# A hybrid convolution decoder layer: from three token blocks in 2 phases to two token blocks in 16 phases, with its long convolution, its PSUM use and its transposes rewritten

## The reference

```
u = rmsnorm(h) * g_mix
proj = u @ w_in                         # 1024 -> 9 x 1024, in this order:
a_b, a_c, a_h, a_z, b_v, b_g, b_z, gate_a, gate_b
s  = a_c * a_h
ya = (a_b * dwconv3(s) * silu(a_z)) @ w_out_a
v  = b_v * sigmoid(b_g)
c  = dwconv31(v) + b_conv_b             # causal, each channel for itself
yb = (silu(layernorm(c)) * silu(b_z)) @ w_out_b
m  = sigmoid(gate_a) * ya + sigmoid(gate_b) * yb
h  = h + m @ w_o
h  = h + sigmoid(rmsnorm(h) @ w_pg) * (p @ w_pe)
y  = rmsnorm(h) * g_final
```

## Time and profile before

| | us |
|---|---|
| three runs | 1177.35, 1189.94, 1219.92 |
| median | 1189.94 |
| span of the profiled execution, slowest core (core 4) | 1170.0 |
| span of the fastest core (core 7) | 1132.5 |
| TensorE busy (share) | 927.0 (79%) |
| VectorE, ScalarE, GpSimd busy (share) | 512.3 (44%), 295.8 (25%), 257.2 (22%) |
| 16 DMA engines: GpSimd's queue, SyncE's queue | 50.9%, 24.7% |

### The profile page before, as it was taken

The page is one execution under the profiler, slowest core; times in us unless marked ns, Lnnn a source line. Parts: engine busy times, 40 slices in busy tenths (PEclk is TensorE's granted clock), DMA queues, the critical chain, the costliest instruction groups (busy, mean ns, idle before and its releaser), DMA issues.

```text
span 1170.0 us, 17595 instructions; the slowest of 8 cores (1132.5 to 1170.0 us)
## 1 busy us (share of the span) xinstructions
PE 927.0 (79%) x6138; PEld 542.0 (46%) x6156; DVE 512.3 (44%) x673; ACT 295.8 (25%) x400; POOL 257.2 (22%) x544
## 2 busy tenths in 40 slices
PE   0799997989866679998898972367768875899995
PEld 0355554645432345555464630124445553566542
DVE  1336556553234433556455231144254653453244
ACT  2122221431143312222242121133111121331143
POOL 3123231222111122222122110011442531111011
PEclk9899998989987898999899996579898897788887
DMA  8999997797522279999899999422899998563001
GB/s 148 188 183 186 177 190 127 120 139 123 92 91 108 87 124 150 165 168 128 95 111 101 99 62 36 112 96 85 146 164 187 172 190 134 89 102 62 1 36 77
DMA packets 101813, 141.98 MB, mean 121 GB/s; under 512 B 42592, under 2 KB 52832, under 8 KB 100704
## 3 DMA queue, kind: packets, MB, share of 16 engines
q0 software_dynamic: 47200, 82.69, 50.9%
q1 hardware_dynamic: 54528, 58.17, 24.7%
HBM read 208.10 MB, written 16.84 MB: 192 GB/s over the span
## 4 chain that ended last, share of the span: by engine, by line
PE 56%; DMA 13%; DVE 12%; issue 6%; ACT 5%; another core or an unknown queue 3%; POOL 2%; SPq 2%; DVEq 0%; POOLq 0%; ACTq 0%
PE ps L467 41%; DMA vd<-t_vt 7%; PE ps L813 5%; DMA t_reg<-vd 4%; PE ps L773 3%; PE ps L575 2%; ACT t_junk L339 2%; PE ps L806 2%; DVE t_reg L831 1%; DVE t_reg L828 1%; SPq L548 1%; DVE t_tmp L696 1%; PE ps L443 1%; DVE t_tmp L700 1%
## 5 line engine op out<-in xcount | busy, mean ns | idle before, releaser
L467 PE MATMUL ps<-t_uT,t_ring 128*128 128x384 bf16 (+1 forms) x3456 | 577.7, 329 | 31.1 <-DVE t_vkeep L532 17.8
L467 PEld LDWEIGHTS ps<-t_uT,t_ring 128*128 128x128 bf16 x3456 | 347.0, 101 | 253.3 <-issue 53.9
L319 POOL DMA_DIRECT2D t_ring<-w_in x216 | 115.3, 538 | 358.2 <-PE ps L467 304.0
L443 PE MATMUL ps<-t_idb,t_xn 128*128 128x128 bf16 x136 | 16.7, 300 | 127.6 <-ACT t_xn L436 94.9
L467 PE MATMUL ps<-t_cbuf,t_ring 128*128 128x384 bf16 (+1 forms) x384 | 70.2, 339 | 9.7 <-DVE t_cbuf L730 9.7
L342 POOL TENSOR_SCALAR t_msq<-t_ssq 128x1 f32<-128x1 f32 x51 | 9.7, 190 | 307.6 <-ACT t_junk L339 307.3
L443 PEld LDWEIGHTS ps<-t_idb,t_xn 128*128 128x128 bf16 x136 | 13.0, 136 | 133.5 <-issue 133.5
L575 PE MATMUL ps<-t_reg,t_ring 128*32 128x384 bf16 (+2 forms) x1024 | 40.0, 311 | 43.4 <-DMA t_reg<-vd 43.4
L737 ACT ACTIVATE t_tmp<-ps 128x768 f32<-128x768 f32 (+1 forms) x48 | 37.1, 772 | 146.2 <-PE ps L467 146.2
L813 PE MATMUL ps<-t_wpg_t,t_u2T 128*128 128x512 bf16 x268 | 73.5, 433 | 0.3
L745 DVE SCALAR_TENSOR_TENSOR t_tmp<-t_tmp,ps 128x768 f32<-128x768 f32 (+1 forms) x30 | 27.3, 910 | 105.2 <-PE ps L467 105.2
(11 more groups left out here) (87 smaller groups left out, 889.7 us busy)
## 6 DMA issues: line engine op xcount, KB each, us to landing
t_ring<-w_in POOLq DMA_DIRECT2D x216, 256.0 KB, 8.9
t_xs<-x SPq DMA_DIRECT2D x34, 512.0 KB, 4.5
y<-t_reg SPq DMA_DIRECT2D x17, 512.0 KB, 2.6
t_ring<-w_cv POOLq DMA_DIRECT2D x24, 256.0 KB, 8.5
t_ring<-w_oa POOLq DMA_DIRECT2D x24, 256.0 KB, 9.8
t_ring<-w_ob POOLq DMA_DIRECT2D x24, 256.0 KB, 6.1
vd<-t_vt SPq DMA_DIRECT2D x16, 200.0 KB, 6.4
t_reg<-vd SPq DMA_DIRECT2D x32, 100.0 KB, 5.6
```

The costliest lines, as they stand in the source:

```text
L319: S.add("pool", lambda e, k=k, src=src: e.dma_start(out=ring[k][:, :], in_=src), reads=after, writes=[f"ring{k}"], dma=f"ring{k}")
L443: S.add("pe", lambda e, i=i, k=k, b=b: e.transpose(out=psb[:, b, k * 128:(k + 1) * 128], in_=xn[i][:, k * 128:(k + 1) * 128], identity=idb ...
L467: S.add("pe", lambda e, b=b, k_=k_, k=k, rhs=rhs, si=si: e.matmul(ps[:, b + si, 0:n], lhsT=ring[k_][:, 128 * k:128 * k + 128], rhs=rhs(k, si),
```

## The change

The program is new; the arithmetic is that of the reference as before.

- **Two blocks** of 1024 and 1152 tokens (the second holds the 128 sample tokens). A unit is 16 matmuls of 512 columns, and in the second block 8 more of 128 columns. All weights are read twice. `unit_u` (operand `uT`) does one chunk of columns after another; `unit_w` (operands `yaT`, `yb`) runs the chunks innermost.
- **PSUM slots**: three of two banks in the first block, two of three banks in the second; banks 6 and 7 are the convolution's. Part of the VectorE work is put in a list (`bg`) and issued in batches by `drain`.
- **16 phases**: a prompt token's place in its block is (token mod 16, token div 16). `vd` has 16 x 128 rows of 66 values (132 bytes), in the second block of 114 (228 bytes), instead of 2 x 128 rows. It comes back in three DMAs of 32 partitions, 64 groups long.
- **Long convolution**: for each pair of channels one matmul with 96x32 weights over 64 columns, 64 of them for a chunk in four column groups; in the second block 64 more over 32 columns for the sample tokens. Each needs no accumulation. Its weights (96 rows of 8 KB in f32) have two buffers of their own, loaded on GpSimd's queue. The result goes through 32x32 transposes on VectorE.
- **Layer norm statistics**: 8 matmuls on quarter tiles, short VectorE and ScalarE work, then one DMA to DRAM and two that broadcast it back to all partitions.
- **Last stage**: apart from the first tile of a block, `u2T` is made by a DMA transpose on SyncE's queue, and so is `uT` of the second block. The products with `w_o` run two tiles ahead. The factor `g_ple` is put into `w_pg`, `g_mix` into the scaling. The last tile of all is done in halves.
- **Start**: eight x tiles are loaded; the weight loads past the third wait for the eighth of them, ahead of the norms' operations on GpSimd's queue. Two units run tile by tile while `uT` is being made.
- **`hist`** is copied from a second copy of the state, in 16 rows of 88 KB, at the start.
- **Other moves**: small copies go from GpSimd to ScalarE; `pT`, `gfin` and the weights of the last stage are loaded into memory that earlier stages used.

The diff, cut to its core:

```diff
-BLOCKS = [
-    dict(row0=0, t0=0, np=384, ns=0),
-    dict(row0=768, t0=384, np=384, ns=0),
-    dict(row0=1536, t0=768, np=256, ns=64),
-]
+NPH = 16
+NCOL = 64
+BLOCKS = [
+    dict(row0=0, t0=0, ns=0, W=2 + NCOL),
+    dict(row0=1024, t0=1024, ns=NS, W=2 + NCOL + 48),
+]
...
-    vd = [nc.dram_tensor(f"vd{i}", [NCH, 2, 128, w], BF16).ap() for i, w in enumerate(WB)]
+    vd = [nc.dram_tensor(f"vd{i}", [NCH, NPH, 128, b["W"]], BF16).ap() for i, b in enumerate(BLOCKS)]
...
+pump(2)
+pump(1, after=["x3"])
+pump(NRING, after=["x7"])
...
+    nslot = 3 if not ns else 2
+    nb = 2 if not ns else 3
+    slot_ctr = [0]
+    chunks = [(0, 512), (512, 1024)] + ([(1024, T)] if ns else [])
+    def salloc():
+        b = (slot_ctr[0] % nslot) * nb
+        slot_ctr[0] += 1
+        return b
...
+    def unit_u():
+        b, k_ = salloc(), wuse()
+        for lo, hi in chunks:
+            for k in range(NCH):
+                mm(b, k_, k, lo, hi, uT, ures(lo, hi))
+        wdone()
...
+        S.add("sp", lambda e: e.dma_start(out=vd[bi][j].rearrange("h p w -> p h w"), in_=vv),
+              reads=vres, writes=[f"vd{j}"], dma=f"vd{v}")
+        flat = vd[bi][j].rearrange("h (c g) w -> (h c) (g w)", c=2)
+        for s in range(3):
+            S.add("sp", lambda e, s=s: e.dma_start(
+                out=R[v][32 * s:32 * s + 32, 0:NCOL * W - s], in_=flat[:, s:NCOL * W]),
+                reads=[f"vd{j}"], writes=[f"R{v}_{s}"], dma=f"R{v}")
...
+    def conv(j):
+        v = j % 2
+        rr = [f"R{v}_{s}" for s in range(3)] + [f"wcv{v}"]
+        for r in range(16):
+            for q in range(4):
+                g = 16 * q + r
+                S.add("pe", lambda e, r=r, q=q, g=g: e.matmul(
+                    psf[32 * q:32 * q + 32, 3072 + 64 * r:3072 + 64 * r + 64],
+                    lhsT=wcv[v][0:96, 32 * g:32 * g + 32], rhs=R[v][0:96, g * W:g * W + NCOL],
+                    start=True, stop=True, tile_position=(0, 32 * q), skip_group_check=True),
+                    reads=rr, writes=["ps6" if r < 8 else "ps7"])
...
+    def conv_s(j):
+        v = j % 2
+        rr = [f"R{v}_{s}" for s in range(3)] + [f"wcv{v}"]
+        for r in range(16):
+            for q in range(4):
+                g = 16 * q + r
+                rhs = R[v][0:96, g * W + 66:g * W + 114].rearrange("p (q c) -> p q c", c=3)[:, :, 0]
+                S.add("pe", lambda e, r=r, q=q, g=g, rhs=rhs: e.matmul(
+                    psf[32 * q:32 * q + 32, 3072 + 32 * r:3072 + 32 * r + 32],
+                    lhsT=wcv[v][0:96, 32 * g:32 * g + 32],
+                    rhs=rhs.unsqueeze(1).to_broadcast([96, 2, 16]),
+                    start=True, stop=True, tile_position=(0, 32 * q), skip_group_check=True),
+                    reads=rr, writes=["ps6"])
...
+    def ln_stats():
+        for q in range(4):
+            for b, src, nm in ((6, accs, "accs"), (7, accq, "accq")):
+                S.add("pe", lambda e, b=b, q=q, src=src: e.matmul(
+                    ps[32 * q:32 * q + 32, b, 0:TQ], lhsT=onesq[:], rhs=src[:, TQ * q:TQ * q + TQ],
+                    start=True, stop=True, tile_position=(0, 32 * q), skip_group_check=True),
+                    reads=["onesq", nm], writes=[f"ps{b}"])
...
+        S.add("sp", lambda e: e.dma_start(out=st_d[bi].rearrange("w (q n) -> q w n", q=4), in_=rn[0:128:32]),
+              reads=[tmr, tmr + "r"], writes=["st"], dma="st")
+        for w, (dst, nm) in enumerate(((accs, "accs"), (accq, "accq"))):
+            S.add("sp", lambda e, w=w, dst=dst: e.dma_start(
+                out=dst[:, 0:T], in_=st_d[bi][w:w + 1, :].to_broadcast([128, T])),
+                reads=["st"], writes=[nm], dma=nm)
...
+    def A_turn_dma(t):
+        sl = t % 2
+        S.add("sp", lambda e: e.dma_start_transpose(out=u2T[sl], in_=xb[sl]),
+              reads=[f"xb{sl}"], writes=[f"u2T{sl}"], dma=f"u2T{sl}")
...
+    def n_turn(n):
+        u, (ap, res) = s6["n", n]
+        sl = n % 2
+        S.add("dve", lambda e: e.scalar_tensor_tensor(
+            out=xn[sl], in0=xs[u % NXS], scalar=ap, in1=gmixb, op0=ALU.mult, op1=ALU.mult),
+            reads=[f"xs{u % NXS}", res, "gmixb"], writes=[f"xn{sl}"])
+        xdone(u)
+        S.add("sp", lambda e: e.dma_start_transpose(out=uT[:, :, 128 * n:128 * n + 128], in_=xn[sl]),
+              reads=[f"xn{sl}"], writes=[f"uT{n}"], dma=f"xn{sl}")
...
+        s = [stats(0)]
+        scale(0, s[0])
+        s.append(stats(1))
+        for t in range(8):
+            if t + 2 < 8:
+                s.append(stats(t + 2))
+            turn(t)
+            if t + 1 < 8:
+                scale(t + 1, s[t + 1])
+            if t >= 1:
+                for i in range(2):
+                    part(i, 128 * (t - 1), 128 * t)
+            if t == 4:
+                part(2, 0, 512)
...
-                S.add("sp", lambda e: e.dma_start(
-                    out=hist_d, in_=sb_d.rearrange("c s (q t) -> c s q t", q=16)[:, :, :, 5:16]), dma="hist")
+        S.add("sp", lambda e: e.dma_start(out=hist_d, in_=sbn_d[:, 8 * D:30 * D]), dma="hist")
...
+    A_mm(0)
+    A_mm(1)
+    A_stt(0)
+    A_xb(0)
+    A_turn_pe(0)
+    A_sq(0)
+    nn = 0
+    for t in range(nt):
+        todo = list(range(nn, nn + next_count(t, nt, len(nxt), nn)))
+        nn += len(todo)
+        if t > 0:
+            G_tanh(t - 1)
+        if t > 0:
+            E1(t - 1)
+            E2(t - 1)
+        if t + 1 < nt:
+            A_stt(t + 1)
+        for n in todo[:1]:
+            n_stats(n)
+        if t + 1 < nt:
+            A_xb(t + 1)
+            A_turn_dma(t + 1)
+        if t > 0:
+            s6["r3", t - 1] = rms_stats(Bbuf[(t - 1) % 2], [f"B{(t - 1) % 2}_0", f"B{(t - 1) % 2}_1"])
+        if t + 1 < nt:
+            A_sq(t + 1)
+        for n in todo[:1]:
+            n_turn(n)
+        if t > 0:
+            D_out(t - 1)
+        for n in todo[1:]:
+            n_stats(n)
+            n_turn(n)
+        pe_mm(t)
+        pg_mm(t, halves=(last and t == nt - 1))
+        if t + 2 < nt:
+            A_mm(t + 2)
```

1172 lines of the change are left out of this document (644 added, 528 removed).

## The result

The changed kernel takes **1104.0 us** (median of four runs, 1100.92 to 1125.71), the kernel before on the same chip 1183.6. The ratio is 0.938, 95% interval 0.934 to 0.943. Run again later on another chip it was 0.930 (0.927 to 0.933) of before, 1085.9 us. The forecast was 980 us, with a range up to 1090. A program on all eight cores has now and then a slower execution; the times given are medians of all runs, while the ratios and the differences between runs leave such executions out.

A forecast was written before the change was run, and what follows sets the result against it. TensorE was taken as the bound: start 63, remaining work 819 and waits (2, 10, 6, 5, 8, 12, 15) make 940 us, with 20 for the clock 960. Runs' median lies 20 above the span: 980 us, range 935 to 1090 (0.84).

The forecast's parts named there:

- TensorE's work, 837: Whole kernel: TensorE's matmuls, transposes, convolution and statistics after the change, priced at full clock, sum to 837 us.
- Start, 63 us: Kernel start: x tiles, 11 weight loads, then eight tiles of transposes end at 63 us, with 18 us of TensorE's work done.
- The DMA term: Convolution stages of both blocks: waiting because DMA work per chunk exceeds TensorE's; 15 us taken, bounds 0 to 172.
- the formula: Convolution stages: with p us for 2048 short runs, the DMA wait is 24p - 126 us.
- Rival 4: Convolution stages: DMA binds at 12.4 us for 2048 short runs, 172 us instead of 15, total 1137 us; chance 0.04.
- Statistics, 10 us: Layer norm statistics: DMA legs and short steps lie under 12 units (41 us); 5 us of waiting per block, 10 us.
- Last stage, 7.8 us a tile: Last stage: 36 matmuls set 7.8 us a tile; nothing waits if the DMA transpose takes at most 6.1 us.
- rival 1: Last stage: DMA transposes come late at 13.3 us each, tiles last 7.2 us longer, total 1088 us; chance 0.12.
- End, 8 us: Kernel end, after the last matmuls: one tile in halves takes 8 us, where two tiles in turn took 17.
- Late stretch at 0.81, 20 us: Late in the kernel: a stretch at 0.81 of full clock, as core 4 had before, adds 20 us.
- rival 3: Whole kernel: TensorE's clock stays at 0.81 throughout, 192 us less the 20 counted, total 1152 us; chance 0.08.
- Rivals 2 and 6: 2: PSUM binds in the second block, 1052 us, chance 0.12. 6: the 708 us standstill comes back, 1018 us, chance 0.02.

The follow-up runs named there:

- the run with the square moved: Changed kernel with the statistics of the tile before put ahead of the next tile's steps in the last stage: 1055.8 us, 0.915 of before.
- the free second store: Changed kernel with the `vd` store issued twice, the second time into an unread place in SBUF: 1080.4 us, 0.933 of before.
- the dear one: Changed kernel with the `vd` store issued twice, the second time into an unread DRAM tensor: 1249.5 us, 1.069 of before.
- with long rows: Changed kernel with the `vd` store as 128 long rows instead of 2048 short runs, values in wrong places: 967.1 us, 0.812 of before.

## Why the prediction was wrong, step by step

The sum was 960 us for a span that came out at 1102.5. In TensorE's terms: 837 us of work and 123 of everything else were forecast (20 of it for the clock), 848 and 254 were found.

- **TensorE's work, 837**: right. 848 busy, with some matmuls at a lower clock (0.84 granted from 55 to 297 us). Eight 128-column products take 0.61 us as taken.
- **Start, 63 us**: right in its order, some 7 us long. The x tiles had landed at 22 us, not 27; GpSimd then issued 11 loads in 5.80 us (5.9 forecast), and the first transpose came at 29.91, not 35. Idle in the first 55 us: 38, against 63 - 18 = 45.
- **The DMA term, "I take 15 (0 to 172)"**: this is the step that failed. With its neighbours (first convolution 2, block-1 start 5, short waits 12) it gave 34 us of idle time in the convolution stages; there were 154, 120 more. That short runs to DRAM would be the wait was in the text. Its size was wrong, and so was the overlap that the formula counts on.

  *The formula.* With the store's price as measured, p = 10.0, for all 24 transfers the formula gives 24 x 10.0 - 126 = 114 in place of 15, so 1079 us, and the kernel ran at 1104 and 1086; but that closeness is luck. Eight of the 24 are state loads, which cost 2.5 to 3.6 us each; priced so, the formula gives 16 x 10.0 + 8 x 3 - 126 = 58. And it takes off 52 us for the 14 tiles that are loaded ahead, as if the weights were what came late. They weren't: GpSimd waited 218 of 242 us for free slots.

  *The wait.* What was late was a chain of landings. I had taken the landing of the store at 6.7 us, within 19 us for the first convolution and 36 for the later ones; it took 29 to 41, with 5 to 8 for the read-back, and at the first convolution, where "I take 2" stood, TensorE idles 22 of the 25 us from 75 to 100. The first block's chunks lasted 30 us (242 / 8) where 22 were forecast, idle 8.5 us each where under 2 was named as the test.

  *The price.* I took 5 us for 2048 runs from the rate of the history copy in two short stretches, 364 to 523 runs in a microsecond, and set aside what the same transfer showed over its whole length, 199 us for 32768 runs, 12.4 us for 2048. The measured 205 runs in a microsecond lie near the second. Why the history copy looked faster in those stretches is in the trace of the kernel before: from 712 to 732 us it ran with no other data packet on the engines, 437 of its packets in a microsecond; from 560 to 700 us, with weights beside it, 29 to 281 in each stretch of 10 us. The rate of a transfer that is alone was applied to one that is not. That isn't all of it: the store with no load beside it took 13.3 us, so a run of the store was dearer than one of the history copy even so, and why stays open.
- **Rival 4 (0.04)** came nearest, 1137 by its price of 12.4 us. It had a chance that didn't fit two bounds of 1.4 and 12.4 with 5 chosen between them, and the range ended at 1090, so it didn't reach the bound that the sum itself had named. A range that took it in, as an unknown cost's bound must be, would have held the time.
- **Statistics, 10 us**: 31. TensorE idles 9.8 us at 297 to 312, 4.7 to 363, and 11.7 and 4.6 in the second block. In the two seams at the start of each (VectorE busy 12.46 of 15 and 16.81 of 18 us) it waits for sums that VectorE still has to make, a backlog of the last chunk's transposes and convolution: work that I had counted under "12 units" lies ahead of them. The chunks of the norm come 3.9 us apart on VectorE. No run tested this; it is read from the rows.
- **Last stage, 7.8 us a tile**: 8.65. The condition that I named, a transpose within 6.1 us, was met (3.7 us), so rival 1 fell. I had costed VectorE's and ScalarE's steps by their sums and not as the ring that they close; the run with the square moved showed the ring and opened it, 7.8 us. TensorE idles 13.4 us in the two last stages and 3.0 in the dense stretch ahead of the second, where 6 were forecast.
- **End, 8 us**: 14.5, for two halves of a tile through the whole chain of gate, statistics and two stores.
- **Late stretch at 0.81, 20 us**: not there. In the dense stretches of 363 to 461 and 902 to 1010 the granted clock is 0.99, so rival 3 fell too. The Trainium skill ("TensorE: Matmul & The Clock Gate", the note on the peak-current limiter) would have the die at 13/16 here; this execution doesn't show it.
- **Rivals 2 and 6**: fell. PSUM appears in none of the long waits, and the standstill is gone with the history copy in long rows.

What stands between sum and span is then -7 (start) + 120 + 21 + 10 + 6.5, some 151 us more idle time, 11 more work, and the 20 not used: 142.

## What to carry to other kernels

Count the short runs that a kernel writes to DRAM, and price them by the worst whole transfer of that kind in the trace, not by a stretch in which it ran alone. If TensorE waits for a chain of transfers, forecast their landing times under traffic and not only the sum of the engines' work. Put the short side of a transposing round trip on the read, and the long rows on the write: same bytes, same number of packets, and here 7% of the time. And where a step's two bounds are ten times apart and its middle is the forecast, the range must reach to the bound.

## What was new about the hardware

- 2048 runs of 132 or 228 bytes from SBUF to DRAM cost the kernel 10.0 us, 5 ns a run, with all eight cores storing; half as many runs of double length 4.9 us less. The same runs into SBUF, partition by partition, cost nothing measurable (0.933 against 0.930 to 0.938 of before), and 2048 runs of 96 bytes read from DRAM into SBUF 2.5 to 3.6 us (an estimate from two ratios).
- One such store with no load beside it landed in 13.3 us, at a DMA share of 0.445; in the changed kernel the first block's stores took 24.0 at the median and up to 41.
- The DMA share alone doesn't show this cost. In the first convolution stage it was 0.89 where the store bound, 0.96 with the free second store and 1.18 with the dear one, against 0.82 with long rows. The GB/s show it better (107, 117 and 94, against 143), and so does share times length: 0.89 x 242 against 0.82 x 185 us, 64 us more of engine time for eight stores.
- SBUF to SBUF, 16 transfers of 128 short runs into two partitions each held SP's queue for 18 to 30 us, at a DMA share of 0.62, with at most 4 of their packets in flight; 32 transfers of 64 runs into one partition each held it for 20 to 23 us, with up to 23.
- A DMA transpose within SBUF landed in 3.7 us (5.3 for the other form) and held SP's queue for 1.2.
